# A hybrid decoder step on one core: two DRAM copies issued in a later stage, and one weight split given to other engines

## The chip, the core and the metric

The kernel runs on one core of one Trainium2 chip. The metric is the device time of one execution in microseconds (us), given as a median of several runs. The engines are PE (TensorE, matrix products; PEld is its weight load), DVE (VectorE), ACT (ScalarE), POOL (GpSimd) and SP (SyncE). In this kernel SP and POOL issue the transfers (DMAs). The core has 16 DMA engines.

## The reference, cut to what matters

One inference step of one decoder layer, for a prompt of 1024 tokens and 8 sample sequences of 4 tokens each:

```
h    = RMSNorm(x) * (1 + scale1(c)) + shift1(c)      # scale, shift, gate: silu(c) @ w_ada
P    = h @ w_in                                      # recurrence | attention | merge gates
yA   = RWKV7(P_rwkv) @ w_pa ; yB = NSA(P_nsa) @ w_pb
x    = x + gate1(c) * ((sigmoid(gA)*yA + sigmoid(gB)*yB) @ w_o)
x    = x + gate2(c) * ConvGLU(RMSNorm(x) * (1 + scale2(c)) + shift2(c))
...
kw_all = concatenate([win_k, kw], 1) ; vw_all = concatenate([win_v, vw], 1)
return ..., kw_all[:, -w_buf:], vw_all[:, -w_buf:]   # the window caches, moved on by 4 tokens
```

So two of the outputs are the cached recent keys and values (8 sequences of 512 rows of 128 numbers each) with the oldest 4 rows dropped and the 4 new ones appended. The 508 old rows of each sequence are copied from input to output as they are.

## The kernel before

Everything is in 32 bits. A product is done in three passes: both operands are split into a high part (a cast to the format that PE takes at speed) and a low part (the rest), and `split_product` (lines 170 to 175) adds high times high, high times low and low times high. A split is therefore a cast and a subtraction; for weights that come through the two-slot ring `w_raw`, `split_block` (line 1658) has POOL do both.

The program is a row of stages. Each is a block in which every engine has its own hand-written list of instructions; between blocks all engines meet. The order around the change:

- `norm_in`: modulation from c, normalisation of the tokens, first products with w_in.
- `project_nsa` (line 438): the attention's columns of w_in, for 9 tiles of up to 128 tokens. PE does per tile i three groups of products (`product`), turns the tile (`turn`), and takes one 2 MB piece of w_ada through `modulation(m)` and `fold(m)`. There is one buffer `wa` for these pieces. SP's list sets their order: piece 0 (`ada(0)`, line 480), its bias row (`gate_bias(0)`, line 485), the two copies of the window caches, DRAM to DRAM (line 496), and then, for each tile, a store of the gate rows (line 490) where there is one, the next piece once PE is done with the last (wait on `ada_mm`), and the tile's outputs (lines 520 to 525).
- `compress` (line 729): compressed keys and values; at its end SP waits for the copies and all outputs of `project_nsa`.
- `attend_prompt` (line 984): the prompt's attention, held by PE, DVE and ACT. Its operands lie on the chip by then; SP loads a table `dist` (line 1091), constants for the next stage (`c_atts`, line 1092), and, after a wait on PE, pages for the next stage (`load_slot`).
- `attend_samples` (line 1265).
- `rwkv` with `rwkv_pairs` (line 1824): the recurrence's 14 blocks of 128 columns of w_in. SP loads blocks 0 and 1, four tables, and stores h to DRAM (`h_scratch`, line 1860); it loads block n once block n-2 is split. ACT casts h in 24 pieces (three spans of 352 tokens by 8 rows of 128, line 1952), DVE subtracts in the same order (line 2023), POOL splits the weight blocks in order (`split_block`, lines 165 and 167). PE's `big(n, i)` takes block n with span i: it waits for `w_split` to reach 2(n+1), and for n = 0 for each piece of h. Block 0 goes to the banks `pA`, the others to `pB`.
- then the recurrence itself (`rwkv_chunks`), the merge, and the feed-forward part.

Of the kernel before, what the change touches and what calls it, by code (L numbers as in the profile page):

```python
# [19 lines left out]
ALU = mybir.AluOpType  # L20
ACT = mybir.ActivationFunctionType
F32 = mybir.dt.float32
# [7 lines left out]
DS = 4  # L30
# [11 lines left out]
WIN = 512  # L42
# [395 lines left out]
def project_nsa(nc, A, S, main, O, gate_dram):  # L438

    with ExitStack() as ctx:  # L440
        sb = lambda n, s: ctx.enter_context(nc.sbuf_tensor(n, s, F32))
        ps = lambda n, s: ctx.enter_context(nc.psum_tensor(n, s, F32))
        sem = lambda n: main.enter_context(nc.semaphore(n))
# [20 lines left out]
            sem("nsa_small_in"), sem("nsa_copied"), sem("nsa_chain"), sem("nsa_summed"),  # L464
            sem("nsa_rooted"), sem("nsa_normed"), sem("nsa_turned"), sem("nsa_evac"))
        out_done = [sem("nsa_out0"), sem("nsa_out1")]
        win_copy = sem("win_copy")
        KCOL, VCOL, KS, VS, KW, VW = 512, 640, 768, 896, 1024, 1152
        outs = [(O["kc"], KCOL), (O["vc"], VCOL), (O["ks"], KS), (O["vs"], VS)]
        wins = [(O["kw"], KW), (O["vw"], VW)]  # L470
        n_out = lambda i: 4 if i < 4 else 6
        with nc.Block() as block:
            @block.sync
            def _(sp):
                sp.dma_start(qf[:, :], A["c_qfac"]).then_inc(load, 16)
                sp.dma_start(kn[:, :], A["norm_rows"]).then_inc(load, 16)
                for k, n in enumerate("kv"):
                    sp.dma_start(S["cpe"][:, k], A[f"cpe_{n}"]).then_inc(S["cmp_pe"], 16)
                def ada(m):
                    sp.dma_start(wa, A["w_ada"][:, 4 + m]).then_inc(wa_in, 16)  # L480

                def gate_bias(m):
                    if gates_to(m):
                        sp.wait_ge(gate_out, 16 * gates_to(m))
                    sp.dma_start(gate_rows[:, :], A["b_ada"][:, (4 + m) * 512:(5 + m) * 512]).then_inc(bias_in, 16)

                def gate_store(m):
                    g0 = 512 * (m % 2)
                    sp.wait_ge(fold_ok, m + 1)
                    sp.dma_start(gate_dram[:, m // 6, g0:g0 + 512], gate_rows[:, :]).then_inc(gate_out, 16)  # L490

                ada(0)
                gate_bias(0)
                for m in range(2):
                    src = (A["win_k"], A["win_v"])[m]
                    sp.dma_start(wins[m][0][1][:, 0:WIN - DS, :], src[:, DS:WIN, :]).then_inc(win_copy, 16)
                for i, (t0, n) in enumerate(TILES):
                    if 1 <= i < 8 and sets[i - 1] == "g":
                        gate_store(i - 1)
                    if 1 <= i < 8 and sets[i] == "g":  # L500
                        gate_bias(i)
                    if i < 7:
                        sp.wait_ge(ada_mm, i + 1)
                        ada(i + 1)
                    if i == 8:
                        sp.wait_ge(mm_done, 9)
                        sp.dma_start(S["cw1"][0][:, :, :], A["cw1_k"]).then_inc(S["cmp_k"], 16)
                        for q in range(2):
                            sp.wait_ge(out_done[q], 16 * sum(n_out(i) for i in range(q, 8, 2)))
                        for kind in range(2):  # L510
                            src = (O["kc"], O["vc"])[kind][0].rearrange("(m r) c -> m r c", r=16)
                            for g in range(2):
                                dst = raw_prompt(S, kind)[:, 1024 * g:1024 * g + 1024]
                                sp.dma_start(dst.rearrange("m (r d) -> m r d", d=HD),
                                             src[:, :, 64 * g:64 * g + 64]).then_inc(S[f"cmp_xp{kind}"], 16)
                    sp.wait_ge(copied, 4 * (i + 1))
                    sp.wait_ge(normed, i + 1)
                    for (op, os), c in outs:
                        dst = op[t0:t0 + n, :] if i < 8 else os[:, :]
                        sp.dma_start(dst, P[0:n, i % 2, c:c + 128]).then_inc(out_done[i % 2], 16)  # L520
                    for (op, os), c in wins:
                        if 4 <= i < 8:
                            sp.dma_start(op[t0 - WIN:t0 - WIN + n, :], P[0:n, i % 2, c:c + 128]).then_inc(out_done[i % 2], 16)
                        if i == 8:
                            sp.dma_start(os[:, WIN - DS:WIN, :], P[0:n, i % 2, c:c + 128]).then_inc(out_done[i % 2], 16)
                gate_store(7)
                S["nsa_out"] = [(out_done[q], 16 * sum(n_out(i) for i in range(q, 9, 2))) for q in range(2)]
                S["nsa_copies"], S["gates_out"] = win_copy, gate_out

            @block.tensor  # L530
            def _(pe):
# [197 lines left out]
def compress(nc, A, S, main, O):  # L729
# [4 lines left out]
    with ExitStack() as ctx:  # L734
# [3 lines left out]
        sem = lambda n: main.enter_context(nc.semaphore(n))  # L738
# [37 lines left out]
        with nc.Block() as block:  # L776
            @block.sync
            def _(sp):
                sp.dma_start(S["table"][:, :], A["page_table"]).then_inc(tab_in, 16)
                sp.dma_start(w1[1][:, :, :], A["cw1_v"]).then_inc(w_in, 16)  # L780
                for k, n in enumerate("kv"):
                    sp.dma_start(w2[:, k], A[f"cw2_{n}"]).then_inc(w_in, 16)
                sp.dma_start(kn[:, :], A["norm_rows"]).then_inc(w_in, 16)
                pages(sp, 0)
                sp.wait_ge(*S["nsa_out"][0])
                sp.wait_ge(*S["nsa_out"][1])
                sp.wait_ge(S["nsa_copies"], 32)
                sp.wait_ge(S["gates_out"], 64)

            @block.gpsimd  # L790
# [190 lines left out]
                        norm_keys(JOBS[j - 1][1])  # L981


def attend_prompt(nc, A, S, main):


    with ExitStack() as ctx:
# [65 lines left out]
        for s in range(NS + 2):  # L1053
# [3 lines left out]
            if s >= 2:  # L1057
                n = s - 2
# [25 lines left out]
        def load_slot(engine, arrived, b, some):  # L1084
            for q in some:
                load_pages(nc, engine, S, A["pool_kv"], b * PAGES + q, S["kv"][slot(b)][:, q, :], S[arrived][slot(b)])

        with nc.Block() as block:
            @block.sync
            def _(sp):  # L1090
                sp.dma_start(dist[:, :], A["c_attp"]).then_inc(tab, 16)
                sp.dma_start(S["c_atts"][:, :], A["c_atts"]).then_inc(S["atts_in"], 16)
                for b in (3, 2, 1):
                    sp.wait_ge(turned, last_turn(free[b]))
                    load_slot(sp, "kv_sp", b, range(PAGES))
                    if b == 2:
                        sp.wait_ge(valued, last_value(free[2]))
                        for w in (1, 3):
                            sp.dma_start(S["kw"][w], A["win_kT"][w]).then_inc(S["kw_in"][w], 16)
                sp.wait_ge(queried, 1)  # L1100
                sp.wait_ge(scored, len(score_at))
                load_slot(sp, "kv_sp", 0, range(0, PAGES, 2))

            @block.gpsimd
            def _(pool):
# [718 lines left out]
def rwkv_pairs(nc, A, S, R, slots, KR, BK, V, O):  # L1824

    with ExitStack() as ctx:
# [7 lines left out]
        w_mm, w_out, a_mm, a_out, sq_out, norm_mm, rooted, inverse, spread_mm, kk_out, scanned, exps, widened, products = (  # L1834
            sem(f"rp_{n}") for n in ("w_mm", "w_out", "a_mm", "a_out", "sq", "norm_mm", "rooted", "inverse", "spread", "kk",
                                     "scanned", "exps", "widened", "products"))
        bonus_mm, bonus_ok, chain = (sem(f"rp_{n}") for n in ("bonus_mm", "bonus_ok", "chain"))
        h_hi, h_lo = S["h_parts"]
        hT, par = S["hT"], S["par"]
        span = lambda i: slice(i * PIECE, (i + 1) * PIECE)  # L1840
# [12 lines left out]
        with nc.Block() as block:  # L1853
# [17 lines left out]

            @block.gpsimd
            def _(pool):
                for n in range(14):
                    if n >= 2:
                        pool.wait_ge(big_mm, n - 1)
                    split_block(nc, pool, S, n)

# [60 lines left out]
            def _(act):  # L1939
# [10 lines left out]
                for i in range(3):  # L1950
                    for q in range(KC):
                        nc.scalar.activation(h_hi[:, q, span(i)], hT[:, q, span(i)], ACT.Copy).then_inc(hi_ready, 1)
                act.wait_ge(R["loads"], 64)
                act.wait_ge(ready, 1)
                for n in range(2):
# [35 lines left out]
            def _(dve):  # L1991
# [10 lines left out]
                def mix(n, dst):  # L2002
                    dve.wait_ge(head_old, n + 1)
                    rwkv_mixed(nc, R, dst, out_of(n), n, slice(0, 2)).then_inc(head_mix, 1)
                    dve.wait_ge(tail_old, n + 1)
                    rwkv_mixed(nc, R, dst, out_of(n), n, slice(2, 3)).then_inc(tail_mix, 1)
                    dve.wait_ge(head_mix, n + 1)
                    dve.wait_ge(tail_mix, n + 1)
# [11 lines left out]
                for i in range(3):  # L2020
                    for q in range(KC):
                        dve.wait_ge(hi_ready, KC * i + q + 1)
                        nc.vector.tensor_tensor(h_lo[:, q, span(i)], hT[:, q, span(i)], h_hi[:, q, span(i)].bitcast(F32),
                                                ALU.subtract).then_inc(h_split, 1)
                mix(0, R["xl"])
                dve.wait_ge(R["h_out"], 16)
                dve.wait_ge(h_split, 3 * KC)
# [1378 lines left out]
def step_kernel(nc, A, OUT):  # L3406

    with ExitStack() as main:
# [18 lines left out]
        with mixes:  # L3427
            S["ybT"] = sb("ybT", [128, 4, T], mixes)
            with ExitStack() as nsa:
# [37 lines left out]
                S["c_atts"] = sb("c_atts", [128, sum(SAMPLE_COLS.values())], nsa)  # L3467
                S["atts_in"] = main.enter_context(nc.semaphore("atts_in"))
                S["qblk"] = sb("qblk", [128, NB, 32], nsa)
                attend_prompt(nc, A, S, main)  # L3470
                attend_samples(nc, A, S, main)
            S["yaT"] = sb("yaT", [128, 4, T], mixes)
            S["ring"] = main.enter_context(ExitStack())
# [101 lines left out]
```

## Time and profile before

| | us |
|---|---|
| median of 3 runs | 2616.39 |
| lowest and highest run | 2614.83 and 2619.54 |
| the profiled execution, as a run | 2620.73 |
| its span, first to last instruction | 2619.1 |
| PE busy in it | 2404.4 |
| DVE, ACT, POOL busy | 1201.2, 785.6, 529.8 |

How to read it: the profile is of one execution. Busy time is the sum of an engine's instructions; the idle time that stands before an instruction is put down to what released it. Times in rows count from the span's start. The granted clock is that of PE, as a share of its full speed (1.00 is 2.4 GHz, 0.50 is 1.2 GHz). PE is busy for 92% of the span, so what matters is where PE stands still, and where it runs at the lower clock.

### The profile page before, as it was taken

The numbers are of one execution on the slowest core, as the hardware profiler recorded it, in microseconds if no ns is written. First come the engines' busy times: TensorE is split into PE (matmuls) and PEld (weight loads), VectorE is DVE, ScalarE is ACT, GpSimd is POOL, SyncE is SP. The second block draws the span as 40 slices with busy tenths as digits, with TensorE's granted clock in tenths as the row PEclk, the third lists the DMA queues.
The fourth block names the chain that finished last, engine by engine and source line by source line (L and its number), as shares of the span: only waits on it lengthen the run. The fifth ranks groups of instructions, "written<-read, shape, count | busy, mean of one in ns | idle before, by whom it ended". The sixth has DMA issues, their size and how long they took to land. (4 is left out here: it accounts for less than half of the span.)

```text
span 2619.1 us, 47668 instructions
## 1 busy us (share of the span) xinstructions
PE 2404.4 (92%) x19959; PEld 2098.2 (80%) x19959; DVE 1201.2 (46%) x2323; ACT 785.6 (30%) x1436; POOL 529.8 (20%) x376
## 2 busy tenths in 40 slices
PE   6898997999856999888998999999999999989998
PEld 4576884444424888888886999977999999989998
DVE  5432225565532334555554544457433333345665
ACT  4232225556612333222222423322111111123332
POOL 4001210000022212000000334341233233223332
PEclk8997898999966999988997999999999999999999
DMA  7445421101244042111003111133211111131221
GB/s 282 176 149 149 142 65 46 33 1 49 66 148 154 25 139 72 70 51 51 7 3 118 48 49 49 45 115 101 60 48 42 49 49 42 48 91 45 78 78 46
DMA packets 160568, 201.60 MB, mean 77 GB/s; under 512 B 14905, under 2 KB 144250, under 8 KB 156834
## 3 DMA queue, kind: packets, MB, share of 16 engines
q1 hardware_dynamic: 154722, 182.81, 21.5%
q0 software_dynamic: 5632, 15.74, 2.1%
q8 instruction: 159, 2.61, 0.4%
q14 instruction: 55, 0.45, 0.1%
HBM read 170.68 MB, written 31.99 MB: 77 GB/s over the span
## 5 line engine op out<-in xcount | busy, mean ns | idle before, releaser
L165 POOL CAST w_hi<-w_raw 128x1024 fp32r<-128x1024 f32 x116 | 132.1, 1139 | 1353.2 <-DMA w_raw<-in_w_in 461.4
L173 PE MATMUL pP_u<-h_hi,w_hi 128*128 128x352 f32 x1056 | 341.0, 323 | 0.3 <-PEq L2943 0.3
L174 PE MATMUL pP_u<-h_lo,w_hi 128*128 128x352 f32 x1056 | 338.6, 321 | 0.0
L175 PE MATMUL pP_u<-h_hi,w_lo 128*128 128x352 f32 x1056 | 338.4, 320 | 0.0
L167 POOL TENSOR_TENSOR w_lo<-w_raw,w_hi 128x1024 fp32r<-128x1024 f32 x116 | 282.4, 2435 | 9.3
L173 PEld LDWEIGHTS pP_u<-h_hi,w_hi 128*128 128x128 f32 x1056 | 198.1, 188 | 0.7 <-issue 0.6
L174 PEld LDWEIGHTS pP_u<-h_lo,w_hi 128*128 128x128 f32 x1056 | 198.5, 188 | 0.0
L175 PEld LDWEIGHTS pP_u<-h_hi,w_lo 128*128 128x128 f32 x1056 | 197.9, 187 | 0.0
L3231 DVE TENSOR_TENSOR conv<-conv,conv_sig 128x1056 f32<-128x1056 f32 x22 | 50.1, 2279 | 312.7 <-ACT conv_sig L3199 312.7
L173 PE MATMUL pP_d<-a_piece_hi,w_hi 128*128 128x352 f32 x528 | 173.3, 328 | 10.5 <-DVE a_piece_lo L3389 8.4
L3398 DVE TENSOR_TENSOR a_piece_lo<-aT,a_piece_hi 128x1408 fp32r<-128x1408 f32 (+1 forms) x71 | 135.7, 1916 | 92.7 <-ACT a_piece_hi L3327 92.7
L175 PE MATMUL pP_d<-a_piece_hi,w_lo 128*128 128x352 f32 x528 | 171.1, 324 | 0.0
L174 PE MATMUL pP_d<-a_piece_lo,w_hi 128*128 128x352 f32 x528 | 171.0, 324 | 0.0
L3327 ACT ACTIVATE a_piece_hi<-aT 128x1408 fp32r<-128x1408 f32 (+1 forms) x71 | 91.0, 1283 | 162.3 <-PE pP_d L175 162.3
L2318 PE MATMUL pB_rc<-rw_work 64*64 64x64 f32 x3632 | 119.5, 222 | 12.1 <-DVE rw_work L2680 8.1
L2318 PEld LDWEIGHTS pB_rc<-rw_work 64*64 64x64 f32 x3632 | 112.4, 137 | 19.4 <-DVE rw_work L2680 8.6
L173 PE MATMUL pG_m<-h_hi,w_hi 128*128 128x352 f32 x384 | 124.6, 325 | 3.5 <-PEq L160 3.5
L174 PE MATMUL pG_m<-h_lo,w_hi 128*128 128x352 f32 x384 | 123.8, 322 | 0.0
L175 PE MATMUL pG_m<-h_hi,w_lo 128*128 128x352 f32 x384 | 123.7, 322 | 0.0
L1221 DVE CUSTOM_DVE_ANT_0 kv_ring<-ps_p,dist_p 128x320 f32<-128x320 f32 (+5 forms) x192 | 92.8, 521 | 64.4 <-PE ps_p L1132 63.6
L173 PE MATMUL pB_e<-h_hi_rw,w_hi 128*128 128x352 f32 x312 | 106.6, 342 | 9.7 <-DVE hT L1802 9.7
L173 PEld LDWEIGHTS pP_d<-a_piece_hi,w_hi 128*128 128x128 f32 x528 | 99.8, 189 | 12.8 <-POOL w_hi L165 7.3
(512 smaller groups left out, 5178.3 us busy)
## 6 DMA issues: line engine op xcount, KB each, us to landing
w_raw<-in_w_up SPq DMA_DIRECT2D x44, 512.0 KB, 4.1
ybT<-in_w_ada SPq DMA_DIRECT2D x9, 2048.0 KB, 8.7
w_raw<-in_w_in SPq DMA_DIRECT2D x30, 512.0 KB, 4.3
kv_ring<-in_pool_kv SPq DMA_DIRECT2D x80, 128.0 KB, 2.2
w_raw<-in_w_down SPq DMA_DIRECT2D x20, 512.0 KB, 3.6
pair_scratch<-hT SPq DMA_DIRECT2D x3, 2752.0 KB, 9.8
cx<-in_pool_c POOLq DMA_DIRECT2D x64, 128.0 KB, 3.0
cx<-in_pool_c SPq DMA_DIRECT2D x64, 128.0 KB, 2.9
```

The lines of the kernel that those rows point to most:

```text
L165: engine.tensor_copy(hi, source).then_inc(done, 1)
L167: engine.tensor_tensor(lo, source, hi.bitcast(F32), ALU.subtract).then_inc(done, 1)
L173: nc.tensor.matmul(out, w_hi, x_hi, start=start, stop=False)
L174: nc.tensor.matmul(out, w_hi, x_lo, start=False, stop=False)
L175: return nc.tensor.matmul(out, w_lo, x_hi, start=False, stop=stop)
L1221: nc.vector.tensor_tensor_reduce(held(n)[:, 4 * g + j, at], pS[:, k % 3, 0:w], table(n)[:, at], 1.0, -3e38, ALU.add, ALU.max, tops[:, n % ...
L2318: mm = nc.tensor.matmul(dst[hr[h], c - 8 * g, :], lhs(hr[h], c), rhs(hr[h], c), start=True, stop=True)
L3231: link(nc.vector.tensor_tensor(c[:, :], c[:, :], sg[:, :], ALU.mult))
L3327: nc.scalar.activation(AR[0][:, m % 3, 0:b - a, :], aT[:, a:b, PIECE * i:PIECE * i + PIECE], ACT.Copy).then_inc(hi_done, 1)
L3398: nc.vector.tensor_tensor(AR[1][:, m % 3, 0:b - a, :], aT[:, a:b, PIECE * i:PIECE * i + PIECE], AR[0][:, m % 3, 0:b - a, :].bitcast(F32), ...
```

## The change

The two copies leave `project_nsa` and are issued by SP at the start of `attend_prompt`, behind `dist` and `c_atts`; the wait for them moves from the end of `compress` to the end of SP's list in `attend_prompt`. In `rwkv_pairs` block 0 of the weights is no longer split by POOL: ACT casts it between its first and its second span of h, DVE subtracts at the same place of its list, behind a new semaphore `first_high`, and raises `w_split` by 2. POOL begins with block 1, once `w_split` is 2.

```diff
@@ project_nsa, SP
                 gate_bias(0)
-                for m in range(2):
-                    src = (A["win_k"], A["win_v"])[m]
-                    sp.dma_start(wins[m][0][1][:, 0:WIN - DS, :], src[:, DS:WIN, :]).then_inc(win_copy, 16)
@@ compress, SP
-                sp.wait_ge(S["nsa_copies"], 32)
@@ attend_prompt, SP
                 sp.dma_start(S["c_atts"][:, :], A["c_atts"]).then_inc(S["atts_in"], 16)
+                for new, old in (("kw", "win_k"), ("vw", "win_v")):
+                    sp.dma_start(O[new][1][:, 0:WIN - DS, :], A[old][:, DS:WIN, :]).then_inc(win_copy, 16)
                 for b in (3, 2, 1):
...
                 load_slot(sp, "kv_sp", 0, range(0, PAGES, 2))
+                sp.wait_ge(win_copy, 32)
@@ rwkv_pairs, POOL
-                for n in range(14):
-                    if n >= 2:
+                for n in range(1, 14):
+                    if n == 1:
+                        pool.wait_ge(S["w_split"], 2)
+                    else:
                         pool.wait_ge(big_mm, n - 1)
                     split_block(nc, pool, S, n)
@@ rwkv_pairs, ACT (in the loop over the spans i of h)
+                    if i == 0:
+                        act.wait_ge(S["w_in"][0], 16)
+                        nc.scalar.activation(S["w_hi"][:, 0, :], S["w_raw"][:, 0, :], ACT.Copy).then_inc(first_high, 1)
@@ rwkv_pairs, DVE (in the loop over the spans i of h)
+                    if i == 0:
+                        dve.wait_ge(first_high, 1)
+                        nc.vector.tensor_tensor(S["w_lo"][:, 0, :], S["w_raw"][:, 0, :], S["w_hi"][:, 0, :].bitcast(F32),
+                                                ALU.subtract).then_inc(S["w_split"], 2)
```

## Rows read from the trace of the kernel before

**Rows 1.** Waits of PE, 100 to 250 us: engine, line, releaser: total, times, longest.
```profile
PE pM L182 <- DMA ybT<-in_w_ada: 11.0, 1, 11.0
```

**Rows 2.** Timeline of `project_nsa`: start, us, engine, line, instruction, [idle before <- releaser].
```profile
82.06 0.43 SPq L480 DMA_DIRECT2D ybT<-in_w_ada  x1
82.97 0.85 SPq L496 DMA_DIRECT2D out_kw_s<-in_win_k  x1
90.83 1.92 PE L182 MATMUL pM<-ybT,cT 128*32 128x512 f32 x16 [0.28 <-DMA ybT<-in_w_ada]
92.68 0.50 PE L173 MATMUL pP<-wn_hi,h_piece_hi 128*128 128x512 f32 x1
...
92.81 0.34 SPq L480 DMA_DIRECT2D ybT<-in_w_ada  x1
...
103.14 0.27 PE L556 MATMUL pTn<-cst,Pn 128*128 128x128 f32 x1
114.38 3.64 PE L182 MATMUL pM<-ybT,cT 128*32 128x512 f32 x16 [10.97 <-DMA ybT<-in_w_ada]
117.95 0.80 PE L173 MATMUL pP<-wn_hi,h_piece_hi 128*128 128x512 f32 x1
```

**Rows 3.** Issue of line 480's 8 loads to landing; then the one of 92.81 us.
```profile
DMA to landing us min/median/max: 7.3/8.5/21.5
ybT<-in_w_ada SPq DMA_DIRECT2D x1, 2048.0 KB, 21.5
```

**Rows 4.** Stretches: busy us (instructions) of PE, PEld, DVE, ACT, POOL; granted clock; DMA share; GB/s.
```profile
112.00:114.00 2.00, 0.00 (x0) 0.00 (x0) 0.00 (x0) 0.00 (x0) 0.00 (x0) 0.50 0.42 165
420.00:430.00 10.00, 10.00 (x49) 4.52 (x46) 7.77 (x30) 6.35 (x14) 0.00 (x0) 1.00 0.00 1
```

**Rows 5.** Timeline, start of `attend_prompt`, and SP's next transfer after it.
```profile
405.98 0.43 SPq L1092 DMA_DIRECT2D c_atts<-in_c_atts  x1
...
410.14 0.22 DVE L1221 CUSTOM_DVE_ANT_0 probs_c<-ps_p,dist_p 128x63 f32<-128x63 f32 x1 [3.23 <-DMA dist_p<-in_c_attp]
...
469.25 157.11 SPq L714 DMA_DIRECT2D kv_ring<-in_pool_kv  x32
```

**Rows 6.** DMA queues, 80 to 92 us: packets, MB, share of 16 engines.
```profile
q8 instruction: 1, 0.02, 0.5%
```

**Rows 7.** Timeline, start of `rwkv_pairs`.
```profile
819.22 9.38 ACT L1952 ACTIVATE h_hi_rw<-hT 128x352 fp32r<-128x352 f32 x24 [0.78 <-PEq L160]
...
819.82 10.54 DVE L2023 TENSOR_TENSOR h_lo_rw<-hT,h_hi_rw 128x352 fp32r<-128x352 f32 x24 [0.34 <-ACT h_hi_rw L1952]
...
823.18 0.45 SPq L1860 DMA_DIRECT2D h_scratch<-hT  x1
823.61 7.64 POOL L165 CAST w_hi<-w_raw 128x1024 fp32r<-128x1024 f32 x1 [32.41 <-DMA w_raw<-in_w_in]
831.34 2.33 POOL L167 TENSOR_TENSOR w_lo<-w_raw,w_hi 128x1024 fp32r<-128x1024 f32 x1
...
833.73 0.66 PE L173 MATMUL pA_e<-h_hi_rw,w_hi 128*128 128x352 f32 x1 [16.12 <-POOL w_lo L167]
...
839.17 0.33 PE L173 MATMUL pA_e<-h_hi_rw,w_hi 128*128 128x352 f32 x1
```

**Rows 8.** The next two POOL casts and a DVE clear between them, in the timeline.
```profile
848.09 1.04 POOL L165 CAST w_hi<-w_raw 128x1024 fp32r<-128x1024 f32 x1 [10.99 <-PE pA_e L175]
850.21 1.87 DVE L2028 MEMSET hT<- 128x2176 f32 x1 [0.57 <-DVE yaT L1802]
859.56 1.04 POOL L165 CAST w_hi<-w_raw 128x1024 fp32r<-128x1024 f32 x1 [7.94 <-PE pB_e L175]
```

**Rows 9.** The same cast and subtraction on ACT and DVE elsewhere: lines 600 and 647, durations in ns.
```profile
L600 ACT ACTIVATE h_piece_hi<-hT x6: 403/1045/1046, 95.7 to 198.1; 128x1024 fp32r<-128x1024 f32 x5, 128x256 fp32r<-128x256 f32 x1
L647 DVE TENSOR_TENSOR h_piece_lo<-hT,h_piece_hi x6: 425/1208/1224, 100.1 to 201.3; 128x1024 fp32r<-128x1024 f32 x5, 128x256 fp32r<-128x256 f32 x1
```

**Rows 10.** DMA issue of the store of h: KB, us to landing.
```profile
h_scratch<-hT SPq DMA_DIRECT2D x1, 4224.0 KB, 17.9
```

More of the change, by code:

```diff
@@ L466, in project_nsa @@
         out_done = [sem("nsa_out0"), sem("nsa_out1")]
-        win_copy = sem("win_copy")
         KCOL, VCOL, KS, VS, KW, VW = 512, 640, 768, 896, 1024, 1152
@@ L527, in _ @@
                 S["nsa_out"] = [(out_done[q], 16 * sum(n_out(i) for i in range(q, 9, 2))) for q in range(2)]
-                S["nsa_copies"], S["gates_out"] = win_copy, gate_out
+                S["gates_out"] = gate_out
             @block.tensor
@@ L981, in _, with attend_prompt @@
                         norm_keys(JOBS[j - 1][1])
-def attend_prompt(nc, A, S, main):
+def attend_prompt(nc, A, S, main, O):
     with ExitStack() as ctx:
@@ L1086, in load_slot @@
                 load_pages(nc, engine, S, A["pool_kv"], b * PAGES + q, S["kv"][slot(b)][:, q, :], S[arrived][slot(b)])
+        win_copy = main.enter_context(nc.semaphore("win_copy"))
         with nc.Block() as block:
@@ L1836, in rwkv_pairs @@
                                      "scanned", "exps", "widened", "products"))
-        bonus_mm, bonus_ok, chain = (sem(f"rp_{n}") for n in ("bonus_mm", "bonus_ok", "chain"))
+        bonus_mm, bonus_ok, chain, first_high = (
+            sem(f"rp_{n}") for n in ("bonus_mm", "bonus_ok", "chain", "first_high"))
         h_hi, h_lo = S["h_parts"]
@@ L3469, in step_kernel @@
                 S["qblk"] = sb("qblk", [128, NB, 32], nsa)
-                attend_prompt(nc, A, S, main)
+                attend_prompt(nc, A, S, main, OUT)
                 attend_samples(nc, A, S, main)
```

## The prediction, as put on record

> **What bounds the kernel now.** PE is busy for 92% of the span, so I first read what PE waited for, stage by stage, and from which stall the two parts of the change could take something. In the stage that issues the copies one wait stands out: PE stood 11.0 us once, before line 182, for a load of w_ada [rows 1]. The timeline shows where: the turn of tile 1 ends at 103.41 us, and `modulation(1)` starts at 114.38 [rows 2]. Its piece had been asked for at 92.81, as soon as PE was done with the piece before, and landed 21.5 us later, where the eight loads of this line take 7.3 to 21.5 us with a median of 8.5 [rows 3]. What is special about this one is what stands ahead of it in SP's list: the two window copies, issued from 82.97 us on [rows 2]. They are 2 x 8 x 508 rows x 512 bytes = 4.16 MB. The load of 82.06, ahead of them, cost PE only 0.28 us [rows 2]. While PE waits, the DMA engines are far from full: at 112 to 114 us their share is 0.42 [rows 4]. So the late load is behind a queue on a part of the engines, not short of bandwidth on all. In the same stretch the granted clock has gone down to 0.50 [rows 4], and the matmuls after the wait are slower: 3.64 us for `modulation(1)` against 1.92 for `modulation(0)`, and 0.80 against 0.50 for the first product after each [rows 2].
>
> In the second stage PE waits 16.12 us for the first `w_lo`, from the end of the stage before to 833.73 [rows 7]. The weights landed by 823.61, when POOL begins to cast; that cast takes 7.64 us, where the casts at 848.09 and 859.56 take 1.04 [rows 7, 8]. It ends at 831.25, 0.9 us after DVE's row of 24 subtractions, which run from 819.82 to 830.36 [rows 7]. That is nearly one plain cast after DVE has gone quiet, so I read it as POOL held off by DVE. After it come 2.33 us of subtraction on POOL.
>
> **The copies leave `project_nsa`.** Without them the load of 92.81 has the life of the other loads: landing at 92.81 + 8.5 = 101.3 by the median [rows 3]. PE asks at 103.41 [rows 2], so nothing of the stall is left, with 2.1 us to spare. Then `modulation(1)` runs as `modulation(0)` did, 92.68 - 90.83 = 1.85 us to the next product [rows 2], which starts at 105.26 in place of 117.95: 12.7 us. The first product gains another 0.80 - 0.50 = 0.30 us from the clock [rows 2]. Sum 13.0 us. Next in line after the stall is PE's own work: line 182's load is the only DMA that PE waited for in 100 to 250 us [rows 1], and all that SP issues later in the stage waits for PE or for a tile's results, so it moves along. The bounds: 11.0 us if the wait alone goes and something else takes the rest, 13.3 if the 0.28 us goes too [rows 2].
>
> **The copies under the prompt's attention.** Here SP issues two more transfers (0.85 us the first [rows 2]) at some 406.4 us, behind `dist` and the constants. Behind them in SP's list is only the wait on PE for pages that are issued at 469.25 [rows 5]; POOL's list is not touched. The engines of DMA are idle in between: share 0.00 at 420 to 430 us [rows 4]. In the first stage the copies were through by 114.4 us at the latest, 31.4 us after their issue and with 4 MB of w_ada beside them [rows 2, 3]. From 406.4 that is 437.8, and 31 us are to spare before 469.25. The cover is thus the attention's compute on data already on the chip; without this cover the copies would hold up the pages. What is ahead of them is `dist`, for which DVE waits 3.23 us [rows 5]: its bounds are nothing, as for the load issued 0.9 us ahead of the copies (0.28 us of PE's time [rows 2]), and the copies' own life of 31.4 us, if it were served along with them. I take nothing, since the first is the same queue, order and copies. The moved wait at the end of SP's list is long met.
>
> The engines' instructions come by DMA too. One such packet came at 80 to 92 us, beside the copies [rows 6], and PE's waits show no price for it [rows 1]. Against this speaks a rule of the Trainium skill, "DMA: Bandwidth & Descriptors", section "Queues, rings and completion order": each engine turns from one queue to another only between packets, and a packet may be many descriptors, so that a small fetch could stand behind a long copy. By this rule the sum would lose what an engine runs dry for, and it is the rival of the slow side below; by the rows it loses nothing.
>
> **Block 0 split by ACT and DVE.** POOL's 7.64 + 2.33 us go. ACT does 8 of its 24 casts first, 9.38 x 8/24 = 3.1 us, to 822.35, then waits for the weights to 823.61 [rows 7], then casts 128x1024 in 1.05 us (line 600 [rows 9]). DVE has done its 8 subtractions by 819.82 + 10.54 x 8/24 = 823.33 and waits; it subtracts in 1.21 us (line 647 [rows 9]). With some 0.1 us for each hand-over PE starts at 823.61 + 1.05 + 0.1 + 1.21 + 0.1 = 826.07 in place of 833.73: 7.7 us. The clock is at its low level at either start; it took 839.17 - 833.73 = 5.4 us of matmuls to get back [rows 7], and I let it take the same.
>
> What is queued behind the two new instructions: ACT's second span starts at 824.66 and ends at 827.8, the third at 830.9; DVE's second span runs from 825.97 to 829.5, the third to 833.0. PE needs the second span after 24 matmuls: 18 at the low clock, (839.17 - 833.73) / 18 = 0.30 us each [rows 7], and 6 at half of that, so at 832.4. All its pieces are there by 829.5: 2.9 us to spare. POOL's block 1 is now its first, from 826. If DVE's 16 subtractions hold it off again, it casts until 833.0 + 0.9 and is done at 833.9 + 2.33 = 836.2. PE has taken 848.06 - 833.73 = 14.3 us for block 0 [rows 7, 8], so it asks at 840.4, and at 826.07 + 11.5 = 837.5 if it ran at the high clock throughout (block 1 took 859.56 - 848.09 [rows 8]). Slack 1.3 to 4.2 us: cost nothing. If POOL gets in first instead, DVE is late by up to 1.04 + 2.33 = 3.4 us, which PE's 2.9 us and its slow pace (0.9 us of matmuls for a piece that DVE makes in 0.44) cover.
>
> The Trainium skill has a rule for this, "SBUF — State Buffer", section "Who interferes with whom": a DVE operation with two SBUF inputs and a POOL operation that reads SBUF lock each other out, for a whole instruction, and who comes first wins. It speaks against the change, in that DVE gets one more such operation and POOL's first split falls among 16 others. By it alone the sum is the same as long as the slack above holds.
>
> The store of h does not move: 823.18 + 17.9 = 841.1 [rows 10]. DVE's clears wait for it; they started at 850.21 [rows 8] and would start at 842.5, so 1.4 us remain. Bounds of this part: 5.4 us (the two operations at twice their rows' time) to 10.2 (7.7, and 2.5 us if the clock were high at once: 18 matmuls at 0.30 in place of 11.5 / 72 = 0.16).
>
> **Sum.** 13.0 + 7.7 = 20.7 us. The profiled execution took 2620.73 us with a span of 2619.1; it would take 2600.0. It stands 4.3 us above the median of the runs, and the stalls are no part of that spread, so I set the sum against the median: 2616.39 - 20.7 = 2595.7 us. The bounds: 11.0 + 5.4 = 16.4 and 13.3 + 10.2 = 23.5, so 2592.9 to 2600.0; the runs of before spread by -1.6 and +3.2 us around their median.
>
> **Rivals.** (a) *Another wait takes the stall's place in `project_nsa`.* ACT stood there for the output of tile 0 as well, and their landing, behind the load ahead of them, would then pace PE. For it speaks only that those outputs sit in the same queue; against it, that PE's next product needs nothing of tile 2. It would give back up to the whole 13.0: 2608.7 at the worst, about 2602 at half. (b) *POOL's block 1 or h's store comes late in `rwkv_pairs`.* It decides once POOL is more than 4.2 us later than worked out; it would give back up to 7.7: 2603.4. (c) *The slow side: an engine's instructions, or `dist`, stand behind the copies in the attention.* It decides when more than 20.7 us are lost there. If the copies hold an engine for all their 31.4 us, PE also loses the 2 us of a restart at the low clock (3.64 - 1.92 + 0.30 [rows 2]): 2595.7 + 33.4 - 3.2 of DVE's wait that is there already [rows 5] = 2625.9. For it speaks the rule above; against it rows 1, 2 and 6. A fetch late by a few us would give 2597 to 2605. (d) *The change doesn't do what it says:* the load of 92.81 was late for another reason, as for 4 MB of outputs or its own place in memory, and the stall stays. Seven loads of the same size and line without it speak against this [rows 3]. It would give 2616.39 - 7.7 = 2608.7.
>
> **How the numbers follow.** The forecast of 2595.7 (2593 to 2600) gets 0.78, (a) 0.06, (b) 0.06, (c) 0.06, of which 0.03 on the slow side, (d) 0.04. The range takes in the bounds, the spread of the runs and the milder halves of (a), (b) and (c): 2591 to 2603. A measurement of this kernel can tell about 0.2%, 5.2 us, from no change: faster by more 0.93, within 0.04, slower by more 0.03.
>
> **What would show it.** In the profile after: line 182's wait for its load gone or under 1 us, all eight loads between 7 and 10 us, and the granted clock at 1.00 from 100 to 120 us; the DMA share at 415 to 440 us no longer 0.00, and no new wait of PE, DVE or ACT there; PE's wait before line 173 in `rwkv_pairs` at about 8.4 us in place of 16.1, the long cast of POOL again near 7 us but with PE at work beside it. The prediction is wrong if the stall at `modulation(1)` stays, if DVE's wait for `dist` grows beyond 3.2 us, or if PE stops between blocks 0 and 1.

## The result, and the profile after

| | before | after |
|---|---|---|
| median, us | 2617.97 (4 runs) | 2597.68 (4 runs) |
| lowest and highest run, us | 2614.83, 2620.62 | 2596.03, 2598.53 |
| span of the profiled execution, us | 2619.1 | 2596.6 |
| PE busy in it, us | 2404.4 | 2394.8 |

The ratio is 0.9927, with a 95% interval of 0.9913 to 0.9940: 20.3 us less by the medians, 16 to 23 by the interval. The forecast was 20.7 us less.

The load of w_ada that was 21.5 us on its way [rows 3] has joined the others, and PE's 11.0 us before line 182 [rows 1] are gone. This is line 479 of the kernel after, which is line 480 of the one before: its issues, who waited for it, and issue to landing.

```profile
L479 SPq DMA_DIRECT2D ybT<-in_w_ada x8: 338/340/432, 86.0 to 193.6; - x8
...
  PE pM L182: 0.2, 1
...
DMA to landing us min/median/max: 7.3/7.8/8.8
```

The timeline of PE there answers to [rows 2], and the stretches (busy us and instructions of PE, PEld, DVE, ACT, POOL, then granted clock, DMA share, GB/s) to [rows 4]; the last two of them lie in the prompt's attention. The DMA share adds up the times of the packets over 16 engines, so it can come out a little above 1.

```profile
107.02 0.27 PE L552 MATMUL pTn<-cst,Pn 128*128 128x128 f32 x1
107.22 1.92 PE L182 MATMUL pM<-ybT,cT 128*32 128x512 f32 x16
```

```profile
108.00:110.00 2.00, 2.00 (x16) 0.93 (x9) 0.79 (x2) 1.97 (x5) 0.00 (x0) 1.00 0.00 0
112.00:114.00 2.00, 2.00 (x10) 1.65 (x9) 1.83 (x7) 1.18 (x2) 0.00 (x0) 1.00 1.07 442
...
410.00:420.00 10.00, 10.00 (x51) 5.03 (x50) 7.88 (x30) 5.16 (x12) 0.00 (x0) 1.00 0.48 204
420.00:430.00 10.00, 8.50 (x35) 3.62 (x34) 7.81 (x28) 4.76 (x12) 0.00 (x0) 1.00 0.15 65
```

`modulation(1)` follows the turn of tile 1 at once and takes 1.92 us in place of 3.64, the clock stays at 1.00, and the load in flight at 112 to 114 us has all the engines. The copies now show as DMA work at 410 to 430 us, where the share was 0.00. The wait of DVE for `dist` there is what it was [rows 5]:

```profile
DVE probs_c L1220 <- DMA dist_p<-in_c_attp: 3.3, 1, 3.3
```

The start of `rwkv_pairs` in the timeline of after, which answers to [rows 7, 8]:

```profile
806.93 3.20 ACT L1954 ACTIVATE h_hi_rw<-hT 128x352 fp32r<-128x352 f32 x8 [0.78 <-PEq L160]
...
811.40 1.06 ACT L1957 ACTIVATE w_hi<-w_raw 128x1024 fp32r<-128x1024 f32 x1 [1.26 <-DMA w_raw<-in_w_in]
...
812.56 1.23 DVE L2032 TENSOR_TENSOR w_lo<-w_raw,w_hi 128x1024 fp32r<-128x1024 f32 x1 [1.45 <-ACT w_hi L1957]
813.71 10.10 DVE L2028 TENSOR_TENSOR h_lo_rw<-hT,h_hi_rw 128x352 fp32r<-128x352 f32 x16
...
813.84 0.66 PE L173 MATMUL pA_e<-h_hi_rw,w_hi 128*128 128x352 f32 x1 [8.52 <-DVE w_lo L2032]
...
814.40 1.16 POOL L165 CAST w_hi<-w_raw 128x1024 fp32r<-128x1024 f32 x1 [35.81 <-DMA w_raw<-in_w_in]
815.64 2.55 POOL L167 TENSOR_TENSOR w_lo<-w_raw,w_hi 128x1024 fp32r<-128x1024 f32 x1
...
829.27 1.87 DVE L2037 MEMSET hT<- 128x2176 f32 x1 [0.70 <-DMA h_scratch<-hT]
...
830.54 1.04 POOL L165 CAST w_hi<-w_raw 128x1024 fp32r<-128x1024 f32 x1 [12.35 <-DMA w_raw<-in_w_in]
```

PE waits 8.52 us in place of 16.12. Two things are not as forecast: POOL's first cast takes 1.16 us and not about 7, and DVE's 16 subtractions take 10.10 us and not 7.0. Two are new: DVE waits 0.70 us for the store of h, and POOL waits for block 2's load, which it had not done.

To see what belongs to which part, the span can be cut at three points that every kernel below has: the first issue of SP in `project_nsa`, the start of `attend_prompt` (SP's first issue there), the issue of block 0 at the start of `rwkv_pairs`, and PE's first product with it.

| kernel | to `project_nsa` | to `attend_prompt` | to `rwkv_pairs` | to block 0's product | to the end |
|---|---|---|---|---|---|
| before | 80.3 | 325.3 | 413.6 | 14.54 | 1785.4 |
| after | 84.2 | 312.4 | 410.3 | 6.94 | 1782.8 |
| e1, copies alone | 83.2 | 311.4 | 410.1 | 14.54 | 1786.5 |
| e2, split alone | 81.7 | 324.9 | 410.1 | 6.92 | 1782.5 |
| e3, no copies | 83.1 | 312.2 | 413.6 | 6.96 | 1784.3 |
| e4, copies first | 82.5 | 311.9 | 433.4 | 6.86 | 1781.8 |
| e5, sixteen engines | 81.9 | 320.5 | 409.9 | 14.54 | 1782.2 |
| e6, small cast | 83.7 | 324.9 | 410.7 | 14.54 | 1783.2 |
| e7, DVE pauses | 79.7 | 325.7 | 408.7 | 7.83 | 1778.7 |
| e8, POOL in mid-row | 83.4 | 312.1 | 410.1 | 6.77 | 1783.9 |
| e9, start together | 83.8 | 324.4 | 409.9 | 8.51 | 1784.3 |
| e10, halves | 81.0 | 311.6 | 412.5 | 5.82 | 1786.3 |

Each row is one profiled execution, in us. The first, third and last columns vary by 4 to 8 us with no regard to the edits (but for e4 in the third). The second and the fourth hardly vary, and tell the parts apart: 324.4 to 325.7 us wherever the copies stay as they were, 311.4 to 312.4 wherever they are gone from this stage; 14.54 us wherever POOL splits block 0 as before, 6.8 to 7.0 wherever ACT and DVE do it whole.

### The profile page after: what moved, and what is told of

Read it like the earlier page. It is cut to its first block and busy times, and to the rows that moved or that the text cites. A ratio compares the mean times of both kernels' runs of the same rounds, so it can differ in the third digit from the quotient of the medians.

```text
span 2596.6 us, 47684 instructions
## 1 busy us (share of the span) xinstructions
PE 2394.8 (92%) x19959; PEld 2092.8 (81%) x19959; DVE 1207.4 (46%) x2324; ACT 786.4 (30%) x1437; POOL 520.0 (20%) x374
## 5 line engine op out<-in xcount | busy, mean ns | idle before, releaser
L165 POOL CAST w_hi<-w_raw 128x1024 fp32r<-128x1024 f32 (+1 forms) x115 | 124.9, 1086 | 1352.3 <-DMA w_raw<-in_w_in 477.3
L167 POOL TENSOR_TENSOR w_lo<-w_raw,w_hi 128x1024 fp32r<-128x1024 f32 (+1 forms) x115 | 280.9, 2443 | 9.2
L3240 DVE TENSOR_TENSOR conv<-conv,conv_sig 128x1056 f32<-128x1056 f32 x22 | 50.2, 2283 | 312.4 <-ACT conv_sig L3208 312.4
L173 PE MATMUL pP_d<-a_piece_hi,w_hi 128*128 128x352 f32 x528 | 173.2, 328 | 10.5 <-DVE a_piece_lo L3398 8.4
```

The lines of the kernel that those rows point to most:

```text
L165: engine.tensor_copy(hi, source).then_inc(done, 1)
L167: engine.tensor_tensor(lo, source, hi.bitcast(F32), ALU.subtract).then_inc(done, 1)
L173: nc.tensor.matmul(out, w_hi, x_hi, start=start, stop=False)
L3240: link(nc.vector.tensor_tensor(c[:, :], c[:, :], sg[:, :], ALU.mult))
```

## The experiments

**e1, the copies alone.** The edit is the change's part in `project_nsa`, `compress` and `attend_prompt`; `rwkv_pairs` stays as it was.

```diff
                 gate_bias(0)
-                for m in range(2):
-                    src = (A["win_k"], A["win_v"])[m]
-                    sp.dma_start(wins[m][0][1][:, 0:WIN - DS, :], src[:, DS:WIN, :]).then_inc(win_copy, 16)
...
+                for new, old in (("kw", "win_k"), ("vw", "win_v")):
+                    sp.dma_start(O[new][1][:, 0:WIN - DS, :], A[old][:, DS:WIN, :]).then_inc(win_copy, 16)
```

> The copies are moved as in the change; block 0 of the recurrence's weights is still split by POOL. Theory (the copies alone made the stall at the second piece of w_ada, and are free under the attention): PE's 11.0 us wait at line 182 is gone, the attention of the prompt starts some 13 us earlier, PE's 16.1 us wait in rwkv_pairs is as before, 2605 us beside 2618 for the kernel before. Rival (the gain of the change came mostly from the second part, or another wait takes the stall's place): less than 6 us faster.

Measured: 2607.37 us beside 2616.82 before, ratio 0.9961 (0.9947 to 0.9975), so 7 to 14 us less. The stall at line 182 is gone and its stage is 13.9 us shorter, as the table has it. In `rwkv_pairs` nothing has moved, to a hundredth (timeline):

```profile
809.17 7.64 POOL L165 CAST w_hi<-w_raw 128x1024 fp32r<-128x1024 f32 x1 [32.00 <-DMA w_raw<-in_w_in]
...
819.29 0.66 PE L173 MATMUL pA_e<-h_hi_rw,w_hi 128*128 128x352 f32 x1 [16.12 <-POOL w_lo L167]
```

**e2, the split alone.** The edit is the change's part in `rwkv_pairs`; the copies stay where they were.

```diff
+                    if i == 0:
+                        act.wait_ge(S["w_in"][0], 16)
+                        nc.scalar.activation(S["w_hi"][:, 0, :], S["w_raw"][:, 0, :], ACT.Copy).then_inc(first_high, 1)
...
+                    if i == 0:
+                        dve.wait_ge(first_high, 1)
+                        nc.vector.tensor_tensor(S["w_lo"][:, 0, :], S["w_raw"][:, 0, :], S["w_hi"][:, 0, :].bitcast(F32),
+                                                ALU.subtract).then_inc(S["w_split"], 2)
```

> The split of block 0 goes to ACT and DVE as in the change; the copies stay in project_nsa. Theory: the 11.0 us wait in project_nsa stays, PE's wait in rwkv_pairs falls from 16.1 to 8.5 us, and with the clock coming back after 3 to 5.4 us of slow matmuls the whole is 7.7 to 9 us faster, about 2610. POOL's first cast: about 1.1 us again, since POOL arrives while DVE passes from one subtraction to the next, and a DVE subtraction is held up in its place. Rival (POOL starved by DVE's row): the cast takes about 7 us again. Rival (what is gained is lost at block 2, which now waits behind the store of h): PE waits at block 2 and the gain is under 4 us.

Measured: 2607.92 us, ratio 0.9968 (0.9957 to 0.9980), so 5 to 11 us less. The wait in `project_nsa` stays at 11.0 us. The timeline of `rwkv_pairs`:

```profile
823.70 0.66 PE L173 MATMUL pA_e<-h_hi_rw,w_hi 128*128 128x352 f32 x1 [8.50 <-DVE w_lo L2033]
...
823.71 1.27 POOL L165 CAST w_hi<-w_raw 128x1024 fp32r<-128x1024 f32 x1 [34.42 <-DVE w_lo L2033]
```

PE gains 7.6 us and does not wait again within blocks 0 and 1; POOL gets in beside DVE's row. By the medians the two parts alone give 9.5 and 8.9 us, 18.4 together, and both at once 20.3: within the intervals they add up.

**e3, no copies at all.**

```diff
-                for new, old in (("kw", "win_k"), ("vw", "win_v")):
-                    sp.dma_start(O[new][1][:, 0:WIN - DS, :], A[old][:, DS:WIN, :]).then_inc(win_copy, 16)
...
-                sp.wait_ge(win_copy, 32)
```

> The changed kernel without the two copies and without the wait for them: the 508 old rows of each sequence's window caches are not written. If the copies cost nothing under the attention, it takes the same as the changed kernel, 2598 us. If they hold up instructions, the table or the pages there, it is faster by what they cost, between 2 and 20 us.

Measured: 2599.18 us, ratio to before 0.9928 (0.9912 to 0.9943), where the change has 0.9927. Taking the copies out altogether brings nothing: under the attention they are free, within the 4 us or so that such a comparison leaves open.

**e4, the copies ahead of `dist`.**

```diff
+                for new, old in (("kw", "win_k"), ("vw", "win_v")):
+                    sp.dma_start(O[new][1][:, 0:WIN - DS, :], A[old][:, DS:WIN, :]).then_inc(win_copy, 16)
                 sp.dma_start(dist[:, :], A["c_attp"]).then_inc(tab, 16)
                 sp.dma_start(S["c_atts"][:, :], A["c_atts"]).then_inc(S["atts_in"], 16)
-                for new, old in (("kw", "win_k"), ("vw", "win_v")):
-                    sp.dma_start(O[new][1][:, 0:WIN - DS, :], A[old][:, DS:WIN, :]).then_inc(win_copy, 16)
```

> The changed kernel with the two copies ahead of the table dist in SP's list in place of behind it. If a queue serves in the order of issue on each engine, dist lands behind the copies: DVE's wait for it grows from 3.3 us to between 15 and 25, and the whole is 12 to 25 us slower than the changed kernel. If engines serve what is at hand side by side, the wait stays under 8 us.

Measured: 2618.86 us in one run, 21 us above the change, all of its gain. The timeline of the stage's start:

```profile
394.44 0.81 SPq L1088 DMA_DIRECT2D out_kw_s<-in_win_k  x1
395.31 0.68 SPq L1088 DMA_DIRECT2D out_vw_s<-in_win_v  x1
396.02 0.43 SPq L1089 DMA_DIRECT2D dist_p<-in_c_attp  x1
...
419.31 0.22 DVE L1220 CUSTOM_DVE_ANT_0 probs_c<-ps_p,dist_p 128x63 f32<-128x63 f32 x1 [23.55 <-DMA dist_p<-in_c_attp]
```

DVE waits 23.55 us in place of 3.3, since `dist` comes through behind the copies. So in this queue what is issued ahead is served ahead, on the engines that it uses: with the copies behind `dist` and `c_atts` the wait is 3.3 us, with the copies ahead of them 20 us more.

**e5, the copies at their old place, on all the engines.** This asks what in the copies made the load late: that they lie on a part of the engines, or their bytes.

```diff
-                    sp.dma_start(wins[m][0][1][:, 0:WIN - DS, :], src[:, DS:WIN, :]).then_inc(win_copy, 16)
+                    cut = lambda t: t.rearrange("b r c -> b (r c)").rearrange("b (x e) -> x b e", x=16)
+                    sp.dma_start(cut(wins[m][0][1][:, 0:WIN - DS, :]), cut(src[:, DS:WIN, :])).then_inc(win_copy, 16)
```

> The kernel before, with the copies at their old place but written with an outermost axis of 16 (16 parts of each sequence) in place of 8 sequences. If the late load of w_ada was due to the copies lying on 8 of the 16 engines, the DMA share is near full until they are through, the load lands after some 13 us in place of 21.5, PE's wait at line 182 falls from 11.0 to 1 to 4 us, and the whole is 7 to 11 us faster than before. If it was the amount of bytes or DRAM, the wait stays at about 11 us and the time the same.

Measured: 2610.88 us beside 2618.29, ratio 0.9977 (0.9967 to 0.9987), so 3 to 9 us less. The loads of line 480 from issue to landing, PE's wait in the timeline, and two stretches while the load is on its way:

```profile
DMA to landing us min/median/max: 7.4/7.8/16.3
```

```profile
110.46 3.64 PE L182 MATMUL pM<-ybT,cT 128*32 128x512 f32 x16 [5.71 <-DMA ybT<-in_w_ada]
```

```profile
100.00:102.00 2.00, 2.00 (x11) 1.27 (x10) 1.16 (x2) 0.00 (x0) 0.00 (x0) 1.00 0.95 309
106.00:108.00 2.00, 0.00 (x0) 0.00 (x0) 0.00 (x0) 0.00 (x0) 0.00 (x0) 1.00 0.94 401
```

Neither expectation holds as it stands. With an outermost axis of 16 the share is 0.94 to 1.07 from 92 to 108 us, when the load has all but landed. Before, it was 0.99 to 1.18 from 96 to 102 us, and only then fell to between 0.22 and 0.60 up to 114 us, of which [rows 4] show the end. The load takes 16.3 us and not 21.5, and 5.3 of the 11.0 us of wait go. The other 5.7 stay, since the bytes still stand ahead.

The single DMA packets in the traces, told apart by their sizes, show how. Before, the copies are 64 packets of 65024 bytes, 8 in flight at any time, and the last ends at 109.0 us. The load's packets come in two halves: 8 in flight beside the copies from 95 to 101 us, none while the copies go on alone, and 8 again from 109 us to its landing. So half of the load passed on engines that the copies left free, and half waited for the copies' end. In e5 the copies are 256 packets of 16256 bytes, 16 in flight, and the last ends at 104.7 us. The edit thus made the packets smaller as well, but that is not the gain: the packets' times add up to 191 us in place of 159. The Trainium skill, "DMA: Bandwidth & Descriptors", section "Why a DMA increments its semaphore by 16 and not by 1", says that a DMA is spread over the largest number of engines up to 16 that divides the slowest axis of both sides: 8 for 8 sequences. The 8 and 16 packets in flight agree with it.

**e6, a small cast ahead of POOL's first.** e1 and e5 show the long cast again (7.64 and 7.46 us), but not whose it is.

```diff
             def _(pool):
+                nc.gpsimd.tensor_copy(first_cast[:, :], par[:, 0:2])
                 for n in range(14):
```

> The kernel before, with one cast of 128x2 numbers as POOL's first instruction of rwkv_pairs, ahead of its wait for the weights. If the 7.64 us of POOL's first cast of block 0 are what POOL pays for its first work after a long pause, the small cast takes 5 to 7 us, the cast of block 0 after it about 1.1 us, and PE starts 3 to 6 us earlier. If DVE's row of subtractions holds POOL off, the small cast is short (DVE has not begun its row), the cast of block 0 again takes 7 to 8 us, and nothing else changes.

Measured: 2618.74 us in one run, as before. The timeline of POOL:

```profile
819.30 0.19 POOL L1875 CAST first_cast<-par 128x2 fp32r<-128x2 f32 x1 [27.89 <-POOLq L160]
823.69 7.65 POOL L165 CAST w_hi<-w_raw 128x1024 fp32r<-128x1024 f32 x1 [4.20 <-DMA w_raw<-in_w_in]
```

The first cast after the pause is short and the one inside DVE's row is long. It isn't the pause by itself; whether it is DVE's row, e7 asks.

**e7, DVE pauses until POOL is through.**

```diff
                     for q in range(KC):
...
+                    if i == 0:
+                        dve.wait_ge(S["w_split"], 2)
```

> The kernel before, with DVE pausing after its first 8 subtractions of h until POOL has split block 0. If DVE's row is what held POOL off, the cast takes 1.1 us and the subtraction 2.3: PE starts some 6.5 us earlier than before (wait of about 9.6 us), with DVE's second span arriving just in time. If the long cast is POOL's own, it takes 7.6 us again and PE's wait stays near 16 us.

Measured: PE's wait falls from 16.12 to 9.40 us, with POOL's operations at their plain times:

```profile
818.39 1.04 POOL L165 CAST w_hi<-w_raw 128x1024 fp32r<-128x1024 f32 x1 [31.75 <-DMA w_raw<-in_w_in]
819.52 2.35 POOL L167 TENSOR_TENSOR w_lo<-w_raw,w_hi 128x1024 fp32r<-128x1024 f32 x1
...
821.92 0.66 PE L173 MATMUL pA_e<-h_hi_rw,w_hi 128*128 128x352 f32 x1 [9.40 <-POOL w_lo L167]
```

So DVE's row it was. The one run took 2603.1 us; by the table 6.7 us of that are this edit's, and the rest lies in columns that vary by themselves. One wait on DVE gives 6.7 of the 7.6 us of the split.

**e8, POOL arrives in the middle of DVE's row.** In the kernel after POOL got in at once, though DVE was at its row as well.

```diff
                         pool.wait_ge(S["w_split"], 2)
+                        pool.wait_ge(h_split, KC + 6)
```

> The changed kernel, with POOL coming to block 1 only after 6 of DVE's remaining 16 subtractions. If POOL gets in between any two of DVE's subtractions, its cast takes 1.1 to 1.6 us as in the changed kernel. If a row that has run for a while shuts it out to its end, as it did in the kernel before, the cast takes about 4.5 us, until 0.9 us after the row's last subtraction, and block 1 is ready some 10 us after PE's start: PE has then run out of block 0 (11.6 to 14 us) or not quite. Total within 3 us of the changed kernel either way.

Measured: 2598.7 us in one run. The timeline:

```profile
812.23 7.05 DVE L2029 TENSOR_TENSOR h_lo_rw<-hT,h_hi_rw 128x352 fp32r<-128x352 f32 x16
...
815.05 5.12 POOL L165 CAST w_hi<-w_raw 128x1024 fp32r<-128x1024 f32 x1 [37.11 <-DVE h_lo_rw L2029]
```

Shut out to the row's end: 5.12 us, until 820.17, and DVE's row ends at 819.28, 0.9 us earlier, as in the kernel before. DVE for its part takes 7.05 us, undisturbed. Block 1 is ready 10.3 us after PE's start, and PE doesn't wait for it.

**e9, POOL and DVE begin together.**

```diff
                     for q in range(KC):
...
+                    if i == 0:
+                        dve.wait_ge(S["w_in"][0], 16)
```

> The kernel before, with DVE's second span held until block 0's weights have landed, so that POOL's cast and DVE's row begin together. If who comes first decides and an early row can be entered, the cast takes 1.1 to 1.6 us, the subtraction 2.5, and PE's wait falls from 16.1 to about 10 us. If DVE's row always wins, the cast takes about 7.5 us again and PE's wait is 16 us or more.

Measured: 2613.64 us in one run; PE's wait is 10.09 us. The timeline:

```profile
822.55 13.08 DVE L2023 TENSOR_TENSOR h_lo_rw<-hT,h_hi_rw 128x352 fp32r<-128x352 f32 x16 [0.24 <-DMA w_raw<-in_w_in]
...
822.58 1.39 POOL L165 CAST w_hi<-w_raw 128x1024 fp32r<-128x1024 f32 x1 [31.83 <-DMA w_raw<-in_w_in]
824.05 2.50 POOL L167 TENSOR_TENSOR w_lo<-w_raw,w_hi 128x1024 fp32r<-128x1024 f32 x1
826.50 1.34 POOL L165 CAST w_hi<-w_raw 128x1024 fp32r<-128x1024 f32 x1
```

POOL gets in, and DVE's row takes 13.08 us. Who is held off goes with when POOL arrives: 0.0 to 1.4 us into DVE's row it got in (after, e2, e9, e10), 2.8 to 4 us into it it did not (before, e1, e5, e6, e8). But time is not what decides: the last row above, POOL's next cast, starts 3.95 us into the row and gets in too. By then DVE had begun only 3 subtractions of the row. By their number the casts do sort: a cast got in when 1 to 4 of them had begun, and was held off when 7 to 10 had.

**e10, block 0 in two halves.** A version that could beat the change: PE starts on the first half.

```diff
-                        nc.scalar.activation(S["w_hi"][:, 0, :], S["w_raw"][:, 0, :], ACT.Copy).then_inc(first_high, 1)
+                        for x in HALVES:
+                            nc.scalar.activation(S["w_hi"][:, 0, x], S["w_raw"][:, 0, x], ACT.Copy).then_inc(first_high, 1)
...
-                        pe.wait_ge(S["w_split"], 2 * (n + 1))
+                        pe.wait_ge(*((S["w_split"], 2 * (n + 1)) if n else (first_half, 1)))
...
+                        if n == 0 and i == 0 and q == 4:
+                            pe.wait_ge(S["w_split"], 2)
```

> The changed kernel, with block 0 cast and subtracted in two halves of 512 columns, and PE starting on the first. PE's wait in rwkv_pairs should fall from 8.5 to 7.4 us and the whole by about 1 us, which a measurement of the whole can't tell from the changed kernel's 2598; the stage's rows can. If PE then waits for the second half, the gain is under 0.5 us.

Measured: 2597.37 us, ratio to before 0.9917 (0.9898 to 0.9935). PE's wait (timeline):

```profile
810.86 0.66 PE L173 MATMUL pA_e<-h_hi_rw,w_hi 128*128 128x352 f32 x1 [7.40 <-DVE w_lo L2037]
```

7.40 us in place of 8.52: 1.1 us in the stage, as expected, and no wait for the second half. In the whole it can't be told from the change.

## Why the prediction was right, point by point

**What bounds the kernel.** Both stalls were the right ones. The copies caused the first: without them (e1, e3) it is gone. One sentence went too far: that the load was late through a queue on a part of the engines, and not for lack of bandwidth. By e5 that is half of it, 5.3 of 11.0 us; the other half is the copies' bytes. The rows that I read, at 112 to 114 us, are the end of the wait; the share from 96 to 102 us (0.99 to 1.18) would have shown the other half. It did not matter to the sum, because the change takes both away.

**The copies leave `project_nsa`.** Forecast 13.0 us. The mean of the table's second column is 325.0 us over the five kernels with the copies as they were (before, e2, e6, e7, e9) and 311.9 over the six without (after, e1, e3, e4, e8, e10): 13.1 us. The steps hold too: the load lands after at most 8.8 us, the wait left is 0.2 us, and `modulation(1)` takes its 1.92 us at the high clock.

**The copies under the attention.** Forecast nothing. e3 agrees, DVE's wait for `dist` is 3.3 us, and the DMA engines are through with them by 426 us. In the kernel after they are issued from 397.5 us on, so they took 28 us where 31.4 were allowed. The order was the ground for taking nothing, and e4 shows that the order makes the difference. The slow rival's price was somewhat high: with `dist` behind the copies the kernel loses 21 us and not 30, which would have ended level with the kernel before and not slower. The rule that a fetch of instructions could stand behind long copies shows no price in these runs: without the copies (e3) and with them (after) the stage lasts 413.6 and 410.3 us, and a price under the 5 us by which this column varies would not show.

**Block 0 split by ACT and DVE.** Forecast 7.7 us, measured 14.54 - 6.94 = 7.6. ACT's cast took 1.06 us (1.05 forecast), DVE's subtraction 1.23 (1.21). The clock came back sooner than the 5.4 us that I let it take: the first product with the short time of 0.32 us starts 3.1 us after the first of all. But over the kernels this is 3.0 us (e3) to 6.3 (e2), with the split on ACT and DVE in both and with POOL's in between (4.8 to 6.0 in before, e1, e5 and e6). So I count it as a spread of single executions and not as the change's.

The step that failed is the one on POOL. I had it wait again for the end of DVE's row, to 836.2 us, with the cast near 7 us. It came 0.69 us into the row, got in at once, and DVE was held off in its place: one subtraction took 1.36 us and the next 2.72, where they take 0.5 (two rows of DVE's timeline in the kernel after):

```profile
814.58 1.36 DVE L2028 TENSOR_TENSOR h_lo_rw<-hT,h_hi_rw 128x352 fp32r<-128x352 f32 x1
...
815.86 2.72 DVE L2028 TENSOR_TENSOR h_lo_rw<-hT,h_hi_rw 128x352 fp32r<-128x352 f32 x1
```

That is the other end that the prediction had priced (DVE late by up to 3.4 us; measured 10.10 - 7.05 = 3.05), and PE's spare time covered it as worked out. With e8, where POOL was shut out as forecast and PE still did not wait, both ends were tried, and both cost nothing.

Two slacks were smaller than stated or missing. DVE's clears had 1.4 us to spare before the store of h and in fact waited 0.70; the next wait on DVE was for ACT, so PE never saw it. And block 2's load, which is now asked for at PE's start, 2.8 us behind the store of h in SP's queue (10.5 us in the kernel before), was not looked at: POOL waits for it to 830.54, and has block 2 split 16.7 + 3.5 = 20.2 us after PE's start, some 4 us before PE is done with block 1. It costs nothing here, but it is the next thing that would.

**Rivals and range.** (a), (b) and (d) are refuted by e1, e2 and the profile after; of (c) the mechanism exists (e4) and the change avoids it by its order. 2597.68 lies 2 us above the forecast of 2595.7, and 1.6 of these are the kernel before itself, whose median is 2617.97 over four runs and was 2616.39 over the three that the forecast started from.

## What to carry to other kernels

A transfer that nobody waits for soon stood ahead of what was issued behind it on the same queue, on the engines that it used (the kernel before, e4): issue it where the queue is idle, and behind the load that a stage starts with. Where a load takes two or three times as long as its like, look at what was issued just ahead of it and at the share of the DMA engines while it is late; a share near one half with an engine waiting meant here that the transfers ahead lay on a part of the engines, and a share near 1 that their bytes were in the way. And where one POOL operation takes many times its usual time, look for a row of DVE operations with two inputs on the chip that ends just before it does: here a short pause in that row (e7), or other engines for the work (e2), gave the time back.

## What the runs showed of the hardware that was not expected

POOL and DVE did not simply take turns. A POOL cast that arrived 2.8 to 4 us into a row of DVE subtractions was held off to the row's end (5.12 us in e8, 7.64 in the kernel before), past 9 (e8) to 15 (before) chances between two subtractions; one that arrived in the row's first 1.4 us went in after at most 0.4 us (1.04 plain; 1.16 in after, 1.27 in e2, 1.35 in e10, 1.39 in e9), and the operations of POOL right behind it went in too, in e9 up to 5.4 us into the row. The Trainium skill, "SBUF — State Buffer", section "Who interferes with whom", has it that whoever comes first holds the shared pair for one whole instruction. The early arrivals agree; for the late ones the runs show a whole row in place of one instruction. Why a cast gets in when up to 4 subtractions of the row have begun, and not when 7 or more have, was not settled.

DRAM-to-DRAM copies of 4.16 MB with an outermost axis of 8 kept the queue from the next load for 21.5 - 7.8 = 13.7 us more than that load alone takes, and with an axis of 16 for 16.3 - 7.8 = 8.5. The load behind the axis of 8 took 21.4 to 21.7 us in every kernel that kept it (before, e2, e6, e7, e9).
